# Causal mask of stick-breaking attention: selections on GpSimd instead of mask matmuls

## The chip, the cores and the metric

The kernel runs on one core of a Trainium2 chip. The metric is the device time of one execution in microseconds. The kernel before took 2844.97 us (median of three runs, 2842.08 to 2851.28).

## The reference, cut to what matters

One inference step of a four-layer trunk, width 1024, on 512 prompt frames and 64 sample frames of a running stream (576 rows in all). Layers 0 and 3 mix with stick-breaking attention, layer 1 with a short gated convolution, layer 2 with gated linear attention; each is followed by a squared-ReLU MLP of 4096 hidden units. The change touches stick-breaking attention alone, 16 heads of 64:

```python
z = einsum('bqhd,bkhd->bhqk', q, k) * 64 ** -0.5
mask = k_pos[None, :] < q_pos[:, None]
log_not = where(mask, log_sigmoid(-z), 0.0)
rev = cumsum(log_not, axis=3, reverse=True)          # over the keys
tail = rev shifted by one key, 0 at the end
a = where(mask, exp(log_sigmoid(z) + tail), 0.0)
out = einsum('bhqk,bkhd->bqhd', a, v)
```

So the mask is needed twice: a masked key adds nothing to the sums over later keys, and its own weight is zero. The prompt attends to itself causally; the 64 sample queries attend to 256 cached keys and causally to their own 64.

## The kernel before, in words

Everything is kept in one program with an instruction order written out by hand for each engine; semaphores order the engines among themselves. Each engine executes its list in order. Projections (line 387) split both operands in a high and a low part and use three matmuls for each product; they take most of the time.

**Units of attention.** Each of the two stick-breaking layers works through 24 units: 8 pairs of heads, and for each pair three blocks of 128 keys, newest first. Unit u has pair u // 3. The index u mod 3 gives the block: 0 is key block 2 with, side by side, key block 3 and the sample's own keys (448 columns of queries a head); 1 is key block 1 and the two cached key blocks (512 columns); 2 is key block 0 (512 columns). A tile of a unit holds keys on the 128 partitions and the queries of both heads side by side in columns, so 896 or 1024 columns. Only the first 128 columns of a unit hold its diagonal block, plus columns 256 to 448 in a unit with u mod 3 = 0 (key block 3's diagonal and the sample's).

**The steps of a unit.**

- `scores` (lines 436 to 468, TensorE): the mask matmuls write minus 1e30 where the key isn't before the query (`masked`, line 444: identity times `maskb`, in bf16), and the scores of queries and keys are added to them in PSUM (`scored`, line 451). It waits until ScalarE has read the PSUM tile's former unit (`a_ready` of u - 3).
- `exponents` and `logs` (lines 865 to 877, ScalarE): exp(z), then ln(1 + e).
- `softplus` (lines 1203 to 1217, VectorE): a clamp that yields the softplus value (line 1209), the high part by a copy in fp32r (line 1213), the low part by a subtraction (line 1215); for u mod 3 = 0 also five small instructions on the newer keys (lines 1222 to 1232).
- `cumulative` (line 477, TensorE): matmuls with triangular and all-ones matrices subtract the sums over later keys from the scores in PSUM. Its high half waits for `sp_hi`, its low half for `sp_lo`.
- `weights` (line 885, ScalarE): exp of the result, into the same SBUF tile; it signals `a_ready`.
- `weighted_values` (line 510, TensorE): values times weights; it waits for `a_ready`.
- `output` (lines 889 and 1237), once a pair: ScalarE's copy and VectorE's low part of the result.

**The order.** TensorE's loop (lines 555 to 560) is scores(k + 2), cumulative(k), weighted_values(k - 1). ScalarE's (lines 910 to 918) is weights(k - 1), output when a pair is done, logs(k + 1), exponents(k + 2). VectorE goes through softplus(u) and puts the output of a pair behind unit 1 of the next. Ahead of the loop TensorE transposes the cached keys (four batches) and the values (ten), and VectorE and ScalarE copy them out in turn.

**GpSimd.** In `stick_breaking` (lines 1641 to 1650) it has three DMAs to issue: the cached values at the start, and the stores of V once all batches are copied. Outside it, it adds squares for the norms (line 1613), makes constants, and works in the convolution and the linear attention.

Of the kernel before, what the change touches and what calls it, by code (L numbers as in the profile page):

```python
# [23 lines left out]
ALU = mybir.AluOpType  # L24
ACT = mybir.ActivationFunctionType

P = 128
# [29 lines left out]
UNITS = 3 * PAIRS  # L57
# [16 lines left out]
def first_slab(layer):  # L74
    return layer * LAYER_SLABS
# [7 lines left out]
def trunk(nc, x_prompt, x_sample, cache_sb_k, cache_sb_v, state_conv, state_gla, norm_mix, norm_mlp, sb_w_qkv, sb_w_o,  # L83
          conv_w_in, conv_w, conv_w_out, gla_w_in, gla_w_gk2, gla_b_gk, gla_norm, gla_w_o, mlp_w_up, mlp_w_down,
          norm_final, y_prompt, y_sample, sb_k_p, sb_v_p, sb_k_s, sb_v_s, conv_p, conv_s, gla_p, gla_s):
    with ExitStack() as ctx:
# [3 lines left out]
        def sem(name):  # L90
            return ctx.enter_context(nc.semaphore(name))
# [8 lines left out]
        big = sb("big", [P, 3 * KC, T], F32)  # L100
# [3 lines left out]
        identb = sb("identb", [P, P], BF16)  # L104
# [3 lines left out]
        maskb = sb("maskb", [P, 192], BF16)  # L108
# [56 lines left out]
        sp_hi, sp_lo, r_ready, a_ready, av_done = (sem(n) for n in ("sp_hi", "sp_lo", "r_ready", "a_ready", "av_done"))  # L165
        nw_sum, nw_hi, nw_lo = sem("nw_sum"), sem("nw_hi"), sem("nw_lo")
# [200 lines left out]
        def _(pe):  # L367
# [64 lines left out]
            def stick_breaking(layer, sb_index):  # L432
# [3 lines left out]
                def scores(u):  # L436
                    p, b, z = u // 3, 2 - u % 3, zduo[u % 3]
                    if u >= 3:
                        pe.wait_ge(a_ready, first + u - 2)
                    if u == 1:  # L440
                        pe.wait_ge(sbt_v, tb // 2 + 1)

                    def masked(e, lo, hi, start):
                        pe.matmul(z[:, e, lo:hi], identb[:], maskb[:, 0:hi - lo], start=start, stop=False,  # L444
                                  skip_group_check=True)

                    def scored(lo, hi, keys, q_lo):
                        for e in range(2):
                            r = slice(HD * e, HD * e + HD)
                            k = keys(r)  # L450
                            mm = pe.matmul(z[0:k.shape[1], e, lo:hi], k, big[r, p, q_lo:q_lo + hi - lo], start=False,  # L451
                                           stop=False, skip_group_check=True)
                        return mm

                    for e in range(2):
                        masked(e, 0, P, True)
                        if b == 2:
                            masked(e, 256, 448, False)
                    if b == 2:
                        scored(0, 256, lambda r: big[r, 8 + p, 256:384], 256)  # L460
                        scored(256, 384, lambda r: big[r, 8 + p, 384:512], 384)
                        scored(384, 448, lambda r: big[r, 8 + p, 512:576], 512).then_inc(z_ready, 1)
                    elif b == 1:
                        scored(0, 384, lambda r: big[r, 8 + p, 128:256], 128)
                        scored(384, 448, lambda r: CKT[r, p, 0:128], 512)
                        scored(448, 512, lambda r: CKT[r, p, 128:256], 512).then_inc(z_ready, 1)
                    else:
                        scored(0, 512, lambda r: big[r, 8 + p, 0:128], 0).then_inc(z_ready, 1)
# [27 lines left out]
                def weighted_values(u):  # L496
                    p, b, a = u // 3, 2 - u % 3, weighted(u)
                    pe.wait_ge(a_ready, first + u + 1)
# [598 lines left out]
        def _(dve):  # L1097
# [102 lines left out]
            def stick_breaking(layer, sb_index):  # L1200
                first = UNITS * sb_index

                def softplus(u):
# [6 lines left out]
                    dve.wait_ge(sp_ready, first + u + 1)  # L1210
# [357 lines left out]
        def _(pool):  # L1568
# [72 lines left out]
            def stick_breaking(layer, sb_index):  # L1641
                evacuated = (BATCHES + KBATCHES) // 2 * sb_index

                pool.wait_ge(chunk_done, 2 * (first_slab(layer) + IN_SLABS) + 3)
                pool.dma_start(CV, cache_sb_v[sb_index, 0].rearrange("(j p) h d -> p j (h d)", p=P)).then_inc(cv_in, 16)
                pool.wait_ge(sbt_v, evacuated + BATCHES // 2)
# [3 lines left out]
                pool.dma_start(sb_v_s[sb_index, 0].rearrange("p h d -> p (h d)"), VT[0:TS, 4, :]).then_inc(kv_stored, 16)  # L1650

# [141 lines left out]
```

## Time and profile before

| | us |
|---|---|
| median of three runs | 2844.97 |
| lowest, highest | 2842.08, 2851.28 |
| profiled execution | 2856.15 |
| its span | 2854.4 |
| TensorE busy | 2811.0 (98%) |
| VectorE busy | 1283.1 (45%) |
| ScalarE busy | 862.5 (30%) |
| GpSimd busy | 220.6 (8%) |
| first attention stage | 176.3 to 299.4 |
| second attention stage | 2248.3 to 2371.4 |

In the profile PE is TensorE's matmuls, PEld its weight loads, DVE is VectorE, ACT ScalarE, POOL GpSimd, SP the engine that issues most DMAs. L444 is line 444 of the kernel. Times in the timeline are microseconds from the start of the span. A busy share over the whole span is a mean over stages that have different limits, so the attention stages have to be read by themselves.

### The profile page before, as it was taken

The page shows a single profiled execution, that of the slowest core. Times are in us where ns is not written, and L with a number is a line of the kernel's source. Part 1 is how long each engine was busy: PE and PEld are TensorE (multiplying, and loading weights), DVE is VectorE, ACT ScalarE, POOL GpSimd, SP SyncE. Part 2 cuts the span into 40 slices and gives each one's busy share as a digit, 9 for nine tenths or more (in the row PEclk, how much of TensorE's full clock was granted, in tenths as well). Part 3 has the DMA queues.
Part 4 walks back from the last instruction along what each step waited for, and adds up shares of the span by engine and source line. Part 5 has one row for each costly group of instructions (what it writes and reads, how often), then busy time and mean ns, then how long its engine had stood idle before and what let it go on. Part 6 is the DMA issues. An engine that isn't in the chain of part 4 may idle for free.

```text
span 2854.4 us, 48946 instructions
## 1 busy us (share of the span) xinstructions
PE 2811.0 (98%) x20946; PEld 2726.8 (96%) x20946; DVE 1283.1 (45%) x1721; ACT 862.5 (30%) x945; POOL 220.6 (8%) x223
## 2 busy tenths in 40 slices
PE   8999999999999999999999999999999999999998
PEld 8986999999999999999999899999999869999998
DVE  4358443333455433334467543433443485433333
ACT  3136332222311322223224432222321363322222
POOL 3000100000111100000133110000010001000001
PEclk9999999999999999999999999999999999999999
DMA  4210232222222222222212122222232102322221
GB/s 153 75 62 1 89 118 78 89 74 89 74 89 74 89 86 77 86 77 89 75 46 73 53 74 89 75 88 82 81 103 74 63 1 89 108 88 81 82 81 56
DMA packets 205497, 223.42 MB, mean 78 GB/s; under 512 B 3750, under 2 KB 200464, under 8 KB 205360
## 3 DMA queue, kind: packets, MB, share of 16 engines
q1 hardware_dynamic: 200992, 206.06, 22.4%
q0 software_dynamic: 4368, 15.38, 1.6%
q8 instruction: 105, 1.72, 0.3%
q14 instruction: 32, 0.26, 0.0%
HBM read 208.56 MB, written 12.86 MB: 78 GB/s over the span
## 4 chain that ended last, share of the span: by engine, by line
PE 96%; ACT 2%; DVE 1%; issue 0%; DMA 0%; ACTq 0%; DVEq 0%
PE bank L387 86%; PE bank L477 3%; PE bank L451 2%; PE bank L621 1%; ACT big L885 1%; PE bank L510 1%; PE bank L444 1%; PE bank L675 0%; PE bank L658 0%; PE bank L573 0%; PE bank L539 0%; PE bank L404 0%; PE bank L674 0%; DVE wlo L1104 0%; PE bank L586 0%; ACT e L885 0%
## 5 line engine op out<-in xcount | busy, mean ns | idle before, releaser
L387 PE MATMUL bank<-ahi,whi 128*128 128x288 f32 x3584 | 773.1, 297 | 7.2 <-DVE alo L1129 7.2
L387 PE MATMUL bank<-alo,whi 128*128 128x288 f32 x3584 | 769.4, 296 | 0.0
L387 PE MATMUL bank<-ahi,wlo 128*128 128x288 f32 x3584 | 768.8, 296 | 0.0
L771 ACT ACTIVATE whi<-raw 128x2048 fp32r<-128x2048 f32 x191 | 364.6, 1909 | 834.3 <-PE bank L387 834.3
L387 PEld LDWEIGHTS bank<-ahi,whi 128*128 128x128 f32 x3584 | 579.8, 189 | 9.3 <-DVE wlo L1104 7.3
L387 PEld LDWEIGHTS bank<-alo,whi 128*128 128x128 f32 x3584 | 579.9, 189 | 0.0
L387 PEld LDWEIGHTS bank<-ahi,wlo 128*128 128x128 f32 x3584 | 579.5, 189 | 0.0
L387 PE MATMUL bank<-hhi,whi 128*128 128x288 f32 x2560 | 550.1, 296 | 1.6 <-DVE hlo L1470 1.6
L387 PE MATMUL bank<-hhi,wlo 128*128 128x288 f32 x2560 | 548.1, 296 | 0.0
L387 PE MATMUL bank<-hlo,whi 128*128 128x288 f32 x2560 | 548.0, 296 | 0.0
L1104 DVE TENSOR_TENSOR wlo<-raw,whi 128x2048 fp32r<-128x2048 f32 x192 | 442.2, 2303 | 202.6 <-ACT whi L771 199.9
L387 PEld LDWEIGHTS bank<-hhi,whi 128*128 128x128 f32 x2560 | 412.5, 189 | 3.5 <-issue 3.4
L387 PEld LDWEIGHTS bank<-hhi,wlo 128*128 128x128 f32 x2560 | 412.8, 189 | 0.0
L387 PEld LDWEIGHTS bank<-hlo,whi 128*128 128x128 f32 x2560 | 412.7, 189 | 0.0
L1514 DVE TENSOR_TENSOR X<-bank,X 128x288 f32 (+1 forms) x320 | 131.7, 453 | 490.6 <-PE bank L387 490.5
L1066 ACT ACTIVATE big<-big 128x576 f32<-128x576 f32 x128 | 87.7, 685 | 547.4 <-DVE big L1531 547.4
L1531 DVE SCALAR_TENSOR_TENSOR big<-bank,rstd 128x288 f32<-128x288 f32 x256 | 105.2, 453 | 230.9 <-PE bank L387 230.8
L1535 DVE TENSOR_TENSOR hlo<-big,hhi 128x576 f32 (+1 forms) x128 | 97.2, 759 | 182.5 <-ACT hhi L1067 182.5
L1177 DVE TENSOR_TENSOR big<-bank,rstd 128x288 f32<-128x288 f32 x152 | 62.4, 452 | 205.4 <-PE bank L387 205.1
L1609 POOL MEMSET big<- 128x576 f32 x8 | 4.6, 578 | 1692.2 <-PE bank L387 1692.2
L802 ACT ACTIVATE ahi<-X,vec (+1 forms) x64 | 49.0, 776 | 243.6 <-DVE X L1514 243.5
L1613 POOL TENSOR_TENSOR big<-big 128x576 f32<-128x576 f32 x63 | 97.7, 1551 | 290.0 <-ACT big L805 290.0
(271 smaller groups left out, 1685.1 us busy)
## 6 DMA issues: line engine op xcount, KB each, us to landing
raw<-in_mlp_w_up SPq DMA_DIRECT2D x64, 1024.0 KB, 5.3
raw<-in_mlp_w_down SPq DMA_DIRECT2D x64, 1024.0 KB, 5.0
raw<-in_sb_w_qkv SPq DMA_DIRECT2D x24, 1024.0 KB, 5.2
raw<-in_conv_w_in SPq DMA_DIRECT2D x12, 1024.0 KB, 5.1
raw<-in_gla_w_in SPq DMA_DIRECT2D x12, 1024.0 KB, 5.4
raw<-in_sb_w_o SPq DMA_DIRECT2D x8, 1024.0 KB, 5.1
out<-mixs POOLq DMA_DIRECT2D x2, 2048.0 KB, 7.7
out<-big POOLq DMA_DIRECT2D x2, 2048.0 KB, 8.2
```

What stands on the lines that cost most here:

```text
L387: mm = pe.matmul(acc[h][:, 0:HALF], w[:, u, k, m * P:(m + 1) * P], a[:, k, h * HALF:(h + 1) * HALF], start=(k == 0 and w is whi and a is a ...
L451: mm = pe.matmul(z[0:k.shape[1], e, lo:hi], k, big[r, p, q_lo:q_lo + hi - lo], start=False, stop=False, skip_group_check=True)
L477: return pe.matmul(z[:, e, lo:hi], sums[:, which, :], src, start=False, stop=False, skip_group_check=True)
L771: act.activation(whi[:, 1 - u], raw[:, 1 - u], ACT.Copy).then_inc(w_hi, 1)
L802: act.activation(at(ahi, j), at(X, j), ACT.Copy, scale=g).then_inc(xg_hi, 1)
L1066: act.activation(sq_h[m], relu_t[m], ACT.Square).then_inc(hid_sq, 1)
L1104: dve.tensor_tensor(wlo[:, u], raw[:, u], whi[:, u].bitcast(F32), ALU.subtract).then_inc(w_lo, 1)
L1177: ins = dve.tensor_tensor(dst, acc, rstd[:, hs], ALU.mult)
L1514: ins = dve.tensor_tensor(part(X, j, hs), bank[2 * m + h][:, 0:HALF], part(X, j, hs), ALU.add)
L1531: ins = dve.scalar_tensor_tensor(relu_t[m][:, hs], bank[2 * m + h][:, 0:HALF], 0.0, rstd[:, hs], ALU.max, ALU.mult)
L1535: dve.tensor_tensor(at(hlo, c), sq_h[m], at(hhi, c).bitcast(F32), ALU.subtract).then_inc(hid_ready, 1)
L1613: pool.tensor_tensor(ssq, ssq, sq_x, ALU.add).then_inc(ssq_add, 1)
```

## The change

The mask matmuls go. The scores of a unit start the accumulation themselves, unmasked. GpSimd sets the masked elements to zero instead, twice a unit, in place, with `affine_select` on the diagonal blocks of both heads: once on the softplus values, between VectorE's line 1209 and line 1213, and once on the weights, between `weights` and `weighted_values`. Two semaphores are new, `sp_masked` and `a_masked`. The scores go on waiting for `a_ready`. The constant `maskb` is still made.

```diff
@@ TensorE, scores
-                    def masked(e, lo, hi, start):
-                        pe.matmul(z[:, e, lo:hi], identb[:], maskb[:, 0:hi - lo], start=start, stop=False,
-                                  skip_group_check=True)
...
-                    for e in range(2):
-                        masked(e, 0, P, True)
-                        if b == 2:
-                            masked(e, 256, 448, False)
                     if b == 2:
-                        scored(0, 256, lambda r: big[r, 8 + p, 256:384], 256)
+                        scored(0, 256, lambda r: big[r, 8 + p, 256:384], 256, True)
...
@@ TensorE, weighted_values
-                    pe.wait_ge(a_ready, first + u + 1)
+                    pe.wait_ge(a_masked, first + u + 1)
@@ VectorE, softplus
                     dve.scalar_tensor_tensor(s, s, LN_MAX, zduo[u % 3][:, :, 0:w], ALU.min, ALU.max).then_inc(sp_ready, 1)
-                    dve.wait_ge(sp_ready, first + u + 1)
+                    dve.wait_ge(sp_masked, first + u + 1)
@@ GpSimd, stick_breaking
+                def causal(u, done):
+
+                    blocks = [(0, P), (256, 384), (384, 448)] if u % 3 == 0 else [(0, P)]
+                    for lo, hi in blocks:
+                        v = weighted(u)[:, :, lo:hi]
+                        ins = pool.affine_select(v, v, [[0, 2], [1, hi - lo]], ALU.is_gt, 0.0, base=0, channel_multiplier=-1)
+                    ins.then_inc(done, 1)
+
+                def softplus_mask(u):
+                    pool.wait_ge(sp_ready, UNITS * sb_index + u + 1)
+                    causal(u, sp_masked)
+
+                def weight_mask(u):
+                    pool.wait_ge(a_ready, UNITS * sb_index + u + 1)
+                    causal(u, a_masked)
+
                 pool.wait_ge(chunk_done, 2 * (first_slab(layer) + IN_SLABS) + 3)
                 pool.dma_start(CV, cache_sb_v[sb_index, 0]...).then_inc(cv_in, 16)
+                softplus_mask(0)
+                softplus_mask(1)
                 pool.wait_ge(sbt_v, evacuated + BATCHES // 2)
                 pool.wait_ge(sbt_a, evacuated + BATCHES // 2)
                 pool.dma_start(sb_v_p[sb_index, 0]...).then_inc(kv_stored, 16)
                 pool.dma_start(sb_v_s[sb_index, 0]...).then_inc(kv_stored, 16)
+                weight_mask(0)
+                for u in range(2, UNITS):
+                    softplus_mask(u)
+                    weight_mask(u - 1)
+                weight_mask(UNITS - 1)
```

## Rows read from the trace of the kernel before

**Rows 1.** The page's chain that ended last: share by engine, then by line.

```profile
PE 96%; ACT 2%; DVE 1%; issue 0%; DMA 0%; ACTq 0%; DVEq 0%
PE bank L387 86%; PE bank L477 3%; PE bank L451 2%; PE bank L621 1%; ACT big L885 1%; PE bank L510 1%; PE bank L444 1%; PE bank L675 0%; PE bank L658 0%; PE bank L573 0%; PE bank L539 0%; PE bank L404 0%; PE bank L674 0%; DVE wlo L1104 0%; PE bank L586 0%; ACT e L885 0%
```

**Rows 2.** Line 444's instructions: durations ns min/median/max, first and last start us.

```profile
L444 PE MATMUL bank<-maskb,identb x128: 219/230/246, 176.3 to 2359.3; 128*128 128x128 bf16 x96, 128*128 128x192 bf16 x32
```

**Rows 3.** Busy time by engine of a stage, a pair, a stretch: PE, PEld, DVE, ACT, POOL, clock.

```profile
176.28:299.40 123.12, 117.83 (x856) 82.18 (x856) 95.67 (x133) 78.10 (x93) 2.15 (x3) 0.99 0.11 39
235.85:249.63 13.78, 13.64 (x101) 9.37 (x100) 11.51 (x17) 9.35 (x11) 0.00 (x0) 1.00 0.00 1
186.00:191.00 5.00, 4.65 (x26) 3.98 (x24) 4.33 (x5) 2.35 (x4) 0.00 (x0) 0.66 0.00 2
```

**Rows 4.** Timeline of PE in one pair: start us, duration us, engine, line.

```profile
235.85 0.45 PE L444 MATMUL bank<-maskb,identb 128*128 128x128 bf16 x4
236.24 1.19 PE L451 MATMUL bank<-big 64*128 64x256 f32 x12
...
240.95 0.29 PE L444 MATMUL bank<-maskb,identb 128*128 128x128 bf16 x2
241.17 0.92 PE L451 MATMUL bank<-big 64*128 64x384 f32 x4
```

**Rows 5.** Timeline of DVE in one pair, with idle time before it.

```profile
241.77 1.09 DVE L1209 SCALAR_TENSOR_TENSOR big<-big,bank 128x896 f32<-128x896 f32 x1 [0.97 <-ACT big L877]
...
246.81 1.22 DVE L1209 SCALAR_TENSOR_TENSOR big<-big,bank 128x1024 f32<-128x1024 f32 x1 [0.50 <-ACT big L877]
...
250.43 0.69 DVE L1237 TENSOR_TENSOR hlo<-bank,hhi 128x512 fp32r<-128x512 f32 x1 [0.41 <-ACT hhi L890]
...
255.55 1.09 DVE L1209 SCALAR_TENSOR_TENSOR big<-big,bank 128x896 f32<-128x896 f32 x1 [0.97 <-ACT big L877]
```

**Rows 6.** GpSimd's selections by shape: busy us, mean ns.

```profile
L1599 POOL TENSOR_SCALAR_AFFINE_SELECT mask<-mask 128x128 f32<-128x128 f32 x1 | 0.3, 292 | 0.1
...
L1599 POOL TENSOR_SCALAR_AFFINE_SELECT mask<-mask 128x64 f32<-128x64 f32 x1 | 0.2, 238 | 0.1
```

**Rows 7.** Timeline where ScalarE releases GpSimd.

```profile
307.70 0.67 ACT L805 ACTIVATE big<-X 128x576 f32<-128x576 f32 x1
...
308.45 1.49 POOL L1613 TENSOR_TENSOR big<-big 128x576 f32<-128x576 f32 x1 [1.75 <-ACT big L805]
```

**Rows 8.** Timeline of DVE and POOL side by side, in the gated linear attention's projection.

```profile
1456.49 2.67 POOL L1711 TENSOR_TENSOR stg<-big,stg 128x1152 f32<-128x1152 f32 x1 [2.30 <-ACT stg L933]
...
1457.03 3.36 DVE L1316 TENSOR_TENSOR stg<-big,stg 128x1152 f32<-128x1152 f32 x1
...
1459.12 3.23 POOL L1699 TENSOR_TENSOR stg<-stg 128x1152 f32<-128x1152 f32 x1
...
1484.97 2.65 POOL L1711 TENSOR_TENSOR stg<-big,stg 128x1152 f32<-128x1152 f32 x1 [8.25 <-ACT stg L933]
...
1485.98 2.26 DVE L1400 TENSOR_SCALAR e<-e 128x1152 f32<-128x1152 f32 x1 [2.40 <-ACT e L973]
```

**Rows 9.** Timeline at the start and the end of the first attention stage.

```profile
185.57 1.09 PE L539 MATMUL bank<-ident,big 128*128 128x128 f32 x8 [2.52 <-DVE mixs L1183]
...
187.01 1.91 PE L539 MATMUL bank<-ident,big 128*64 128x128 f32 x8 [0.35 <-DVE mixs L1183]
...
195.92 1.22 POOL L1648 DMA_DIRECT2D out<-mixs  x1 [19.26 <-ACT mixs L845]
...
196.15 0.69 DVE L1213 CAST hlo<-stg 128x1024 fp32r<-128x1024 f32 x1
...
197.13 0.55 POOL L1650 DMA_DIRECT2D out<-mixs  x1
...
200.42 1.09 DVE L1209 SCALAR_TENSOR_TENSOR big<-big,bank 128x896 f32<-128x896 f32 x1 [2.32 <-ACT big L877]
...
294.69 1.23 DVE L1215 TENSOR_TENSOR split_q<-big,split_q 128x1024 fp32r<-128x1024 f32 x1
```

More of the change, by code:

```diff
@@ L165, in trunk @@
         sp_hi, sp_lo, r_ready, a_ready, av_done = (sem(n) for n in ("sp_hi", "sp_lo", "r_ready", "a_ready", "av_done"))
+        sp_masked, a_masked = sem("sp_masked"), sem("a_masked")
         nw_sum, nw_hi, nw_lo = sem("nw_sum"), sem("nw_hi"), sem("nw_lo")
@@ L441, in scores, with scored @@
                         pe.wait_ge(sbt_v, tb // 2 + 1)
-                    def masked(e, lo, hi, start):
-                        pe.matmul(z[:, e, lo:hi], identb[:], maskb[:, 0:hi - lo], start=start, stop=False,
-                                  skip_group_check=True)
-                    def scored(lo, hi, keys, q_lo):
+                    def scored(lo, hi, keys, q_lo, start=False):
                         for e in range(2):
@@ L450, in scored @@
                             k = keys(r)
-                            mm = pe.matmul(z[0:k.shape[1], e, lo:hi], k, big[r, p, q_lo:q_lo + hi - lo], start=False,
+                            mm = pe.matmul(z[0:k.shape[1], e, lo:hi], k, big[r, p, q_lo:q_lo + hi - lo], start=start,
                                            stop=False, skip_group_check=True)
                         return mm
-                    for e in range(2):
-                        masked(e, 0, P, True)
-                        if b == 2:
-                            masked(e, 256, 448, False)
                     if b == 2:
-                        scored(0, 256, lambda r: big[r, 8 + p, 256:384], 256)
+                        scored(0, 256, lambda r: big[r, 8 + p, 256:384], 256, True)
                         scored(256, 384, lambda r: big[r, 8 + p, 384:512], 384)
@@ L463, in scores @@
                     elif b == 1:
-                        scored(0, 384, lambda r: big[r, 8 + p, 128:256], 128)
+                        scored(0, 384, lambda r: big[r, 8 + p, 128:256], 128, True)
                         scored(384, 448, lambda r: CKT[r, p, 0:128], 512)
@@ L467, in scores @@
                     else:
-                        scored(0, 512, lambda r: big[r, 8 + p, 0:128], 0).then_inc(z_ready, 1)
+                        scored(0, 512, lambda r: big[r, 8 + p, 0:128], 0, True).then_inc(z_ready, 1)
                 def cumulative(u):
```

## The prediction, made before the changed kernel was run

> **What bounds the kernel now.** I read the chain of waits first [rows 1]: 96% of it is TensorE, 86% the projection matmuls of line 387, and only 1% the mask matmuls of line 444. The diff touches nothing outside the two attention stages, so what matters is the limit inside them. The mask matmuls are 128 in number and lie in those two stages [rows 2]; the first stage takes 123.1 us, and a period inside it (one pair of heads, three units) takes 13.78 us, with TensorE busy 13.64, VectorE 11.51, ScalarE 9.35 and GpSimd nothing at all [rows 3]. So TensorE sets the pace of a pair today, by a small margin. I write 0, 1, 2 for a unit by its index modulo 3.
>
> VectorE's margin comes from the timeline of one pair [rows 5]. Its period, softplus to softplus of unit 0, is 255.55 - 241.77 = 13.78 us. In it VectorE waits 0.50 + 0.41 + 0.97 = 1.88 us, for ScalarE's logarithms and for its copy of the output. That leaves 13.78 - 1.88 = 11.90 us of work that VectorE must issue in order. This 11.90 is the number on which the case turns.
>
> **The change part by part.** *Removed: mask matmuls.* In each pair TensorE loses four before unit 0's scores and two before each other unit's. From start to start that is 236.24 - 235.85 = 0.39 us and 241.17 - 240.95 = 0.22 us, the last twice (unit 2's look the same) [rows 4]: 0.83 us a pair, 13.3 us over 16 pairs. TensorE's period would be 13.78 - 0.83 = 12.95 us, if TensorE stayed the one that sets it. The scores still wait for the unmasked weights, so nothing is added in front of them.
>
> *Added: the selections' own time.* GpSimd took 0.292 us for 128 columns and 0.238 for 64 [rows 6]: 0.054 us for 64 more columns, 0.184 fixed. A block of both heads is 256 columns: 0.184 + 4 x 0.054 = 0.40 us. Units 1 and 2 have one block; unit 0 has two and one of 2 x 64 columns, 0.40 + 0.40 + 0.29 = 1.10 with rounding. That is 1.90 us a pair for the softplus values and 1.90 for the weights. Upper end: if 256 columns cost twice 0.292, 0.58 + 0.58 + 1.46 = 2.6 us. Lower end: 0.238 for each of five, 1.2 us. I take 1.90, the line through the two rows.
>
> The Trainium skill (GPSIMD Engine Reference, section on elementwise work, side-by-side cycle accounting) states 1.8 cycles at 1.2 GHz, 1.5 ns, an element for a one-input loop. Laid on the fixed 0.184 that gives 0.57 us for 256 columns and 2.7 for the pair's softplus masks instead of 1.9, some 2890 us for the kernel, the case C below. It would also give 0.38 us for 128 columns where the row shows 0.29, so here the row decides.
>
> *Added: a wait inside VectorE's softplus.* The copy to the high part (line 1213) now waits for GpSimd, which waits for line 1209. VectorE is in order: behind the waiting copy stand the low part, unit 0's five newer-key instructions, the output's low part and the next softplus; nothing fills the hole. So the 1.90 us are not hidden under VectorE's other work, they are added to it. Two hand-overs come with each unit: an instruction of ScalarE that ended at 308.37 released GpSimd at 308.45, 0.08 us [rows 7]; for the way back I estimate 0.04, about what separates an ending ScalarE instruction from the next engine. Of this 0.03 is spent already between lines 1209 and 1213. 3 x 0.09 = 0.27 us a pair. Ends: 0 to 0.6.
>
> *Added: the two engines on one path to SBUF.* GpSimd started a two-input instruction at 1456.49 that ended at 1459.16; VectorE's began at 1457.03 and took 3.36 us, 1.23 of it after that end; GpSimd's next, of 3.23 us, ran 1.96 of them after VectorE's end at 1460.39 [rows 8]. They took turns, each held for the whole of the other. A VectorE instruction with one input, 1152 columns, was held too: begun at 1485.98, done 0.62 us after GpSimd's end at 1487.62 [rows 8]. The masks of the weights fall in this trap. GpSimd's order is softplus mask of u, weight mask of u - 1. In the pace of VectorE the weights of u - 1 are done when the softplus mask of u ends: TensorE's last sums and ScalarE's exponential take about 2.3 us behind the low part of u - 1, and VectorE needs as long or longer (1.25 for line 1209, then the mask). So the weight mask starts just as the high copy of u is released, and the copy waits 0.40 us behind it in two of three units; for unit 0's three selections, taking turns, both the copy and the low part wait, 0.8. Full price 1.6 us a pair; nothing if VectorE wins each race. I take 1.3, near the full price, because GpSimd's next instruction follows without a gap (1459.12 on an end at 1459.16). Ends: 0 to 2.6.
>
> *The new period.* 11.90 + 1.90 + 0.27 + 1.30 = 15.4 us, over TensorE's 12.95 and over today's 13.78. ScalarE's 9.35 fits. VectorE then waits for nobody else: after the low part of a unit, last sums, exponential and logarithm take 3.3 us, and VectorE has at least 4.8 to do (output, softplus with its mask, copies). The 0.83 us taken from TensorE are worth nothing here.
>
> *Start of a stage.* TensorE's transposes wait for VectorE there (2.52 us) [rows 9], and softplus of units 0 and 1 stands in front of the copies that free them. The first mask costs 1.10 + 0.09, less 0.39 of mask matmuls: +0.8; the second +0.5. Then unit 2: GpSimd first issues the stores of V (1.22 + 0.55 us from 195.92, now from 197.2 to 199.0), then unit 0's weight mask (1.10), and only then unit 2's softplus mask, to 200.5. The high copy, today at 196.15, comes at 200.55, its low part ends at 202.5, and unit 3's softplus, today at 200.42 after 2.32 us idle [rows 9], begins at 202.5: +2.1 us. That idle time absorbs the rest of the delay.
>
> *The seven periods after it.* From 200.42 to the end of the last low part (294.69 + 1.23 = 295.92 [rows 9]) there are 95.5 us today, with seven pairs of softplus. New: 7 x 15.4 = 107.8, +12.3. *End:* the last weight mask is in the open, 0.40 + 0.12 = +0.5.
>
> *Sum.* 12.3 + 2.1 + 0.5 = 14.9 us a stage, 29.8 for two. The profiled execution took 2856.15 us (span 2854.4, 1.75 around it); it would take 2886, +1.04%. On the median of 2844.97, from which I count, that is 2875 us.
>
> **The rivals.** *A: VectorE wins the race, or the selections do not hold it.* For it: the two sides start within 0.1 us of each other. Against: [rows 8]. Period 14.07, so 3.0 + 2.1 + 0.5 = 5.6 us a stage, 2856 us.
>
> *B, the other side: VectorE's idle time swallows the masks and TensorE keeps the pace.* Place: the hole between lines 1209 and 1213. The whole saving of 0.83 us a pair then counts, 13.3 us, less 2 us of start: 2834 us. It decides at a period of 12.95, which is 1.05 us of stall a pair; five selections at 0.2 and three hand-overs already exceed this. No change within my bound would need 1.4 to 2.0 us of stall in all; the selections and hand-overs alone are 2.2. Only VectorE's 1.88 us of idle speak for it, and they are counted.
>
> *C: the selections over the two heads cost 256 columns at the full double price.* 2.6 us for the stall and half of its extra for collisions: period 16.4 to 16.7, about 22 to 24 us a stage, 2890 us.
>
> *D: TensorE's clock falls.* With 12.95 us of work in 15.4 it gets gaps. At the start of the stage the granted clock was 0.66 in 5 us [rows 3] after a pause of TensorE; inside a pair it was 1.00. Eight transposes took 1.91 us there instead of 1.09 [rows 9], on its way between 1.2 and 2.4 GHz; at that ratio, 1.75, a pair of 12.95 takes 22.7. If a third of the pairs ran so, 5 x 7.3 = 37 us more, 2912 us. Against: the new gaps are of about 0.8 us, three a pair, and today's of 0.2 leave it whole.
>
> **How the numbers follow.** Forecast 0.52, A 0.22, B 0.04, C 0.14, D 0.05, others 0.03. A measurement here tells about 0.3% (8.5 us) from nothing. Faster: B, 0.04. Same: a third of A with shorter selections, and strays, 0.09. Slower 0.87. The range goes from A to the midst of C's far side: 2854 to 2898.
>
> **What would show it.** In the changed trace, inside a stage: a period of 15.4 us; VectorE idle between lines 1209 and 1213 for 1.2 us in unit 0 and 0.5 in the others, released by GpSimd; selections of 0.40 us in the hole and longer ones behind it; line 1213's mean above 0.69; TensorE waiting on VectorE's parts at line 477 and no longer on ScalarE at the scores; granted clock 1.00. Wrong would be: VectorE still idle for ScalarE (rival B), line 1213 at 0.69 (A), selections of 0.58 (C). Outside the stages nothing should move by more than 1 us.

## The result, and the profile after

The changed kernel took 2868.88 us (median of eight runs, 2856.72 to 2872.13), the kernel before 2852.81 us (eight runs, 2841.6 to 2860.74) on the same chip: ratio 1.0056, 95% interval 1.0032 to 1.008. It is slower by 0.56%, about 16 us. The forecast was slower, by 1.04% or 29.8 us, so the difference that came is about half of it; the forecast time, 2875 us, lies 6 us above what came. The profiled execution of the changed kernel took 2869.93 us, with a span of 2868.2, that is 13.8 more than the 2854.4 of before.

The chain that ended last, from the page of the changed kernel; it answers to [rows 1]:

```profile
PE 90%; DVE 6%; issue 1%; POOL 1%; ACT 1%; DMA 0%; ACTq 0%; POOLq 0%; DVEq 0%
```

TensorE's share fell from 96 to 90%, and VectorE's rose from 1 to 6%: VectorE is now the limit inside the two attention stages. (In the kernel after, the lines of the attention's engines stand 7 lower: the clamp is line 1202, the high copy 1206, the low part 1208, the first newer-key instruction 1215, the sums 470, the weighted values 503, the logarithms 870, the weights 878. The selections are line 1642.)

Who waited for the selections of line 1642, by the view of that line (us, times):

```profile
  DVE whi L1206: 17.1, 24
  DVE hlo L1206: 8.3, 6
  DVE split_r L1206: 7.5, 10
  DVE split_q L1206: 5.3, 8
```

38.2 us in 48 waits of VectorE between clamp and high copy, in the two stages. The same hole in one pair, by VectorE's timeline; it answers to [rows 5]. The bracket is the idle time before an instruction and who ended it:

```profile
243.96 1.07 DVE L1202 SCALAR_TENSOR_TENSOR big<-big,bank 128x896 f32<-128x896 f32 x1
246.15 0.63 DVE L1206 CAST whi<-big 128x896 fp32r<-128x896 f32 x1 [1.12 <-POOL big L1642]
...
247.82 0.63 DVE L1215 TENSOR_TENSOR raw<-big 128x256 f32<-128x256 f32 x1
...
249.69 1.21 DVE L1202 SCALAR_TENSOR_TENSOR big<-big,bank 128x1024 f32<-128x1024 f32 x1
251.41 0.87 DVE L1206 CAST whi<-big 128x1024 fp32r<-128x1024 f32 x1 [0.51 <-POOL big L1642]
252.32 1.30 DVE L1208 TENSOR_TENSOR wlo<-big,whi 128x1024 fp32r<-128x1024 f32 x1
...
254.28 1.20 DVE L1202 SCALAR_TENSOR_TENSOR e<-e,bank 128x1024 f32<-128x1024 f32 x1
256.00 0.69 DVE L1206 CAST split_q<-e 128x1024 fp32r<-128x1024 f32 x1 [0.51 <-POOL e L1642]
256.72 1.31 DVE L1208 TENSOR_TENSOR split_q<-e,split_q 128x1024 fp32r<-128x1024 f32 x1
257.95 1.07 DVE L1202 SCALAR_TENSOR_TENSOR big<-big,bank 128x896 f32<-128x896 f32 x1
```

Three things are to be seen. The period is 257.95 - 243.96 = 13.99 us, where it was 13.78 [rows 5]. All waits for ScalarE are gone; the only idle time left is 1.12 + 0.51 + 0.51 = 2.14 us, and all of it is GpSimd's. And a few instructions are longer than they were: the copy takes 0.87 in one unit where it took 0.69, the first newer-key instruction 0.63 where it took 0.42.

GpSimd's side of the same pair, by its timeline (a row can hold several selections, x3 or x4, with their time together):

```profile
245.10 1.01 POOL L1642 TENSOR_SCALAR_AFFINE_SELECT big<-big 128x256 f32<-128x256 f32 x3 [2.14 <-DVE big L1202]
246.85 1.31 POOL L1642 TENSOR_SCALAR_AFFINE_SELECT big<-big 128x256 f32<-128x256 f32 x1 [0.74 <-ACT big L878]
250.97 2.81 POOL L1642 TENSOR_SCALAR_AFFINE_SELECT big<-big 128x256 f32<-128x256 f32 x4 [2.80 <-DVE big L1202]
255.55 0.41 POOL L1642 TENSOR_SCALAR_AFFINE_SELECT e<-e 128x256 f32<-128x256 f32 x1 [1.77 <-DVE e L1202]
256.13 0.82 POOL L1642 TENSOR_SCALAR_AFFINE_SELECT big<-big 128x256 f32<-128x256 f32 x1 [0.17 <-ACT big L878]
```

A selection on 2 x 128 columns takes 0.41 us while VectorE stands still (the row of 255.55), three of unit 0 take 1.01. Beside VectorE's copies and low parts the same ones take 0.82 and 1.31.

Busy time by engine of the same pair, and of a stretch at the end of the first stage (columns: length, PE, PEld, DVE, ACT, POOL, granted clock, DMA share, GB/s); they answer to [rows 3]:

```profile
243.96:257.95 13.99, 13.07 (x94) 8.96 (x93) 11.68 (x17) 9.27 (x12) 6.37 (x10) 1.00 0.00 0
295.00:300.00 5.00, 4.99 (x28) 3.77 (x27) 4.40 (x6) 1.02 (x1) 2.33 (x3) 0.66 0.00 0
```

TensorE now has 0.9 us of idle time in a pair and keeps its full clock in it. At the end of the stage it doesn't: the granted clock of that stretch is 0.66.

**Where the 13.8 us are.** I measure a stage from GpSimd's issue of the cached values' DMA to its first constant after the stage, since both stand in its list before and after. The first stage went from 130.19 to 135.27 us (+5.08), the second from 130.46 to 137.21 (+6.75). Its parts, by VectorE's rows: start (DMA to the clamp of unit 3) +1.54 and +1.83; from there to the end of the last low part 97.99 and 98.00 where it was 95.50 in both, +2.49 and +2.50; the rest, end of the stage, 11.26 and 12.63 us where it was 10.21 in both, +1.05 and +2.42. Together +11.83. The other 2.0 us arose in layer 2, which the change doesn't touch: between the two constants of GpSimd that stand around it (1337.31 and 1638.88 in the trace of before) lie 301.57 us before and 303.48 in the changed kernel, and over the twelve traces of this case 299.3 to 304.1 us, in no order that follows the masks. In 23 runs of the kernel before that went beside the experiments the whole time lay between 2834.24 and 2860.24, so single total times tell little here, and the experiments are read by the length of stage and period in their traces.

### The profile page after: what moved, and what is told of

It reads as the page before. It is cut to its first block, busy times and chain, and to the rows that moved or that the text cites. A ratio compares the mean times of both kernels' runs of the same rounds, so it can differ in the third digit from the quotient of the medians.

```text
span 2868.2 us, 48850 instructions
## 1 busy us (share of the span) xinstructions
PE 2807.5 (98%) x20818; PEld 2725.2 (95%) x20818; DVE 1285.4 (45%) x1721; ACT 861.5 (30%) x945; POOL 316.2 (11%) x383
## 4 chain that ended last, share of the span: by engine, by line
PE 90%; DVE 6%; issue 1%; POOL 1%; ACT 1%; DMA 0%; ACTq 0%; POOLq 0%; DVEq 0%
PE bank L388 86%; DVE big L1202 1%; PE bank L614 1%; POOL big L1642 1%; DVE whi L1206 1%; DVE wlo L1208 0%; PE bank L470 0%; DVE e L1202 0%; PE bank L668 0%; PE bank L651 0%; PE bank L566 0%; DVE raw L1215 0%; DVE hlo L1230 0%; PE bank L405 0%; DVE split_r L1206 0%
```

## The experiments

The theory going in was the prediction's with smaller sizes: VectorE's list sets the pace; a period is its work, plus the holes in which it waits for GpSimd, plus what the weight selections hold it up. The rivals were that TensorE's clock or order, or GpSimd's own length, sets the 13.99.

### No selections at all (x_none)

Takes the waits and all selections out of the changed kernel, so nothing is masked:

```diff
-                    pe.wait_ge(a_masked, first + u + 1)
+                    pe.wait_ge(a_ready, first + u + 1)
-                    dve.wait_ge(sp_masked, first + u + 1)
+                    dve.wait_ge(sp_ready, first + u + 1)
-                softplus_mask(0) ... weight_mask(UNITS - 1)
```

> The changed kernel without any selection: neither softplus values nor weights are masked, no engine waits for GpSimd; the output lacks the causal mask. It shows what the removed mask matmuls are worth alone. Theory (VectorE's in-order work with the hole for the selections sets the changed kernel's pace; without the hole TensorE sets it): period of a pair 12.95 us (13.78 less 0.83), stage about 123.1 - 6.6 = 116.5 us. Rival (the score matmuls get no cheaper, or ScalarE sets the pace through the weights): period within 0.2 of 13.78.

Measured: period 12.97 us (12.95 to 12.98 over both stages), stages 124.25 and 124.51 us, that is 5.9 less than before in each; 2847.32 us in one run. VectorE's timeline of one pair:

```profile
239.39 1.09 DVE L1202 SCALAR_TENSOR_TENSOR big<-big,bank 128x896 f32<-128x896 f32 x1 [0.57 <-ACT big L870]
...
244.21 1.22 DVE L1202 SCALAR_TENSOR_TENSOR big<-big,bank 128x1024 f32<-128x1024 f32 x1 [0.28 <-ACT big L870]
...
247.62 0.69 DVE L1230 TENSOR_TENSOR hlo<-bank,hhi 128x512 fp32r<-128x512 f32 x1 [0.20 <-ACT hhi L883]
...
252.36 1.09 DVE L1202 SCALAR_TENSOR_TENSOR big<-big,bank 128x896 f32<-128x896 f32 x1 [0.58 <-ACT big L870]
```

VectorE waits for ScalarE again, as before, and TensorE is busy 55.35 us of the 56 from 215 to 271: it sets the pace. So the 0.83 us of mask matmuls a pair were sized rightly (13.78 - 12.95), and they are worth 12 us over two stages (260.65 - 248.76 = 11.9) if nothing takes the matmuls' place. The selections cost 23.7 us over this (272.48 - 248.76).

### The softplus values' selections alone (x_softplus)

The weights stay unmasked: `weight_mask` isn't called, and `weighted_values` waits for `a_ready`.

> The changed kernel with the softplus selections only; the weights aren't masked, so no selection runs beside VectorE's copies. Theory: VectorE still sets the pace, and the period falls from 13.99 by what the collisions with the weight selections cost, 0.55 us as line 1206, 1208 and 1215 grew: 13.44 us; line 1206 at 0.69, line 1208 at 1.23 again. Rival (the collisions cost the 1.3 us of the prediction): 12.95, TensorE's own pace.

Measured: period 13.45 us (13.44 to 13.46), stages 130.91 and 130.56, 2856.25 us in one run. VectorE's timeline of one pair:

```profile
237.91 1.08 DVE L1202 SCALAR_TENSOR_TENSOR big<-big,bank 128x896 f32<-128x896 f32 x1
240.10 0.63 DVE L1206 CAST whi<-big 128x896 fp32r<-128x896 f32 x1 [1.12 <-POOL big L1642]
...
241.77 0.42 DVE L1215 TENSOR_TENSOR raw<-big 128x256 f32<-128x256 f32 x1
...
243.09 0.43 DVE L1225 TENSOR_TENSOR split_r<-raw,split_r 128x256 fp32r<-128x256 f32 x1
243.44 1.21 DVE L1202 SCALAR_TENSOR_TENSOR big<-big,bank 128x1024 f32<-128x1024 f32 x1
245.16 0.69 DVE L1206 CAST whi<-big 128x1024 fp32r<-128x1024 f32 x1 [0.51 <-POOL big L1642]
245.89 1.23 DVE L1208 TENSOR_TENSOR wlo<-big,whi 128x1024 fp32r<-128x1024 f32 x1
...
251.35 1.08 DVE L1202 SCALAR_TENSOR_TENSOR big<-big,bank 128x896 f32<-128x896 f32 x1
```

Every instruction has its old length again (0.69, 1.23, 0.42), the holes are the same 2.14 us. So VectorE's own work issued back to back is 13.45 - 2.14 = 11.31 us, not 11.90, and the weight selections' effect on VectorE in the changed kernel is 13.99 - 13.45 = 0.54 us a pair. The lengthened instructions give the same: +0.18 (copy of unit 1), +0.08 and +0.08 (low parts of units 1 and 2), +0.21 (line 1215), in all 0.55. The whole is then 11.31 + 2.14 + 0.55 = 14.00.

### The weights' selections alone (x_weights)

The other half: the softplus values stay unmasked, the copy waits for the clamp alone, and GpSimd's list after the stores is `for u in range(UNITS): weight_mask(u)`.

> The changed kernel with the weight selections only; the softplus values aren't masked and VectorE has no hole. Theory: the weight selections have slack of 2.7 to 4 us before TensorE needs them, so they cost nothing: period 12.95 us like the kernel without selections, although VectorE's copies are held a little. Rival (the collisions, or TensorE's wait for masked weights, set the pace): 13.5 us or more.

Measured: period 12.95 to 12.99 us, the first one 13.8; stages 126.36 and 126.35; 2842.09 us in one run. That is TensorE's pace: the selections of the weights cost a period nothing while VectorE has time to spare, and what they add to the path from weights to values is hidden. The stages are 2.1 and 1.8 us longer than in x_none all the same: 0.7 and 0.4 at the start (24.53 and 24.55 us from the DMA to the clamp of unit 3, 23.83 and 24.11 without them), 0.9 in the one longer period and behind it, and 0.5 at the end, where the last selection is in the open.

### Twice the softplus selections (x_double)

Ahead of each selection of softplus values the same selections once more, into an unused tile:

```diff
                 def softplus_mask(u):
                     pool.wait_ge(sp_ready, UNITS * sb_index + u + 1)
+                    for w in (P, P, TS) if u % 3 == 0 else (P,):
+                        made(pool.affine_select(conv_y[:, 0:2 * w]..., negones[:, 0:w]..., [[0, 2], [1, w]], ...))
                     causal(u, sp_masked)
```

> The changed kernel with, before each softplus selection, one more of the same size by GpSimd on scratch. It doubles the hole. Theory: everything GpSimd adds between lines 1202 and 1206 is added to the period: four times 0.36 + 0.08 and once 0.25 + 0.08, so 2.1 us a pair: period 16.1, stage about 128.2 + 7 x 2.1 + 2 = 145 us; TensorE gets gaps of over 1 us in each unit, and its clock may fall in some. Rival (there is slack that absorbs part, as the small rise of 0.21 us a pair suggests): period under 15.5.

Measured: period 16.14 to 16.37 us, stages 154.65 and 153.58, 2895.82 us in one run. VectorE's copies:

```profile
242.32 0.80 DVE L1206 CAST whi<-e 128x896 fp32r<-128x896 f32 x1 [2.43 <-POOL e L1642]
...
248.03 0.87 DVE L1206 CAST hlo<-big 128x1024 fp32r<-128x1024 f32 x1 [0.99 <-POOL big L1642]
...
```

The third copy of the pair waits 0.99 us too. The holes grew from 2.14 to 2.43 + 0.99 + 0.99 = 4.41 us, and the period by about as much (2.2 to 2.4): what GpSimd does between clamp and copy comes through to the period in full. Over the changed kernel's stages these are 19.4 and 16.4 us more, where 16.7 were expected; of the 19.4, 15.8 lie in the pairs, 2.6 at the start (28.6 against 26.02) and 1.0 at the end. From 215 to 271 the mean granted clock was 0.88 here, where it is 1.00 in the changed kernel: rival D exists, but with longer pauses of TensorE (up to 1.44 us, at 248.96) than the change makes inside a pair (0.79).

### Hiding the selection under the clamp (x_split)

The clamp is cut in two, the columns with the diagonal blocks first; GpSimd masks them while VectorE clamps the others.

```diff
-                    dve.scalar_tensor_tensor(s, s, LN_MAX, zduo[u % 3][:, :, 0:w], ALU.min, ALU.max).then_inc(sp_ready, 1)
+                    near = slice(256, w) if u % 3 == 0 else slice(0, P)
+                    rest = slice(0, 256) if u % 3 == 0 else slice(P, w)
+                    for part_, done in ((near, sp_ready), (rest, sp_rest)):
+                        dve.scalar_tensor_tensor(s[:, :, part_], s[:, :, part_], LN_MAX, zduo[u % 3][:, :, part_],
+                                                 ALU.min, ALU.max).then_inc(done, 1)
+                    dve.wait_ge(sp_rest, first + u + 1)
```

> The changed kernel with VectorE's softplus (line 1202) cut in two: the columns of the diagonal block first, GpSimd is released, and the rest of the columns while GpSimd selects. In unit 0 the columns 256 to 448 go first and the block 0 to 128 is selected last. Theory (the hole is VectorE waiting, nothing else): the hole goes from 0.51 to about 0 in units 1 and 2 and from 1.12 to about 0.5 in unit 0; three more instructions cost some 0.3 us; VectorE's period 13.99 - 2.14 + 0.5 + 0.3 = 12.7, under TensorE's 12.97, so the period is 12.97 to 13.1 and the stage some 126 to 128 us from the DMA of line 1654 to the memset of line 1602 (changed kernel 135.3 and 137.2, before 130.2). Kernel about 8 us faster than before. Rival (GpSimd and VectorE also hold each other up during line 1202, or GpSimd's selections now fall on copies): period stays near 14.

Measured: 2848.91 us (median of ten), ratio to the kernel before 0.9989, interval 0.9968 to 1.001; stages 125.54 and 126.55 us. VectorE's timeline of one pair (line 1205 is the clamp, 1211 the copy):

```profile
240.17 1.15 DVE L1205 SCALAR_TENSOR_TENSOR big<-big,bank 128x384 f32<-128x384 f32 x2 [0.52 <-ACT big L870]
241.89 0.63 DVE L1211 CAST whi<-big 128x896 fp32r<-128x896 f32 x1 [0.57 <-DVE big L1205]
...
245.34 1.28 DVE L1205 SCALAR_TENSOR_TENSOR big<-big,bank 128x256 f32<-128x256 f32 x2
246.70 0.69 DVE L1211 CAST whi<-big 128x1024 fp32r<-128x1024 f32 x1
...
253.12 1.15 DVE L1205 SCALAR_TENSOR_TENSOR big<-big,bank 128x384 f32<-128x384 f32 x2 [0.51 <-ACT big L870]
```

The two pieces of the clamp take 1.28 us together where one took 1.21. The hole has gone in units 1 and 2 and is 0.57 in unit 0, where the copy comes 0.09 us after GpSimd's three selections end (the row names the clamp; the selections ran from 240.79 to 241.80). The period is 253.12 - 240.17 = 12.95: TensorE's, as in the prediction. The two stages are 20.4 us shorter than in the changed kernel and 8.6 shorter than in the one before. This shows the hole to be the cause of the slowdown: the same selections in the same number cost 3.3 us over the two stages (252.09 against 248.76 without any) where they cost 23.7, once VectorE doesn't stand still for them, and what is left lies at the start and the end of a stage. In the total the gain over the kernel before is not told from no change by the interval.

### The start of a stage (x_start)

`softplus_mask(2)` and `weight_mask(0)` go ahead of the two stores of V in GpSimd's list.

> The changed kernel with unit 2's softplus mask and unit 0's weight mask put ahead of the two DMAs that store V in GpSimd's order. Theory: at the start of a stage VectorE waited 2.55 us before line 1206 of unit 2; with this it waits 0.51, but unit 3's softplus then waits for ScalarE's logarithm (about 1.3 us after the low part), so about 1.0 to 1.3 us less a stage. Rival: the start is set by ScalarE and TensorE and nothing changes (under 0.3 us).

Measured: from the DMA to the clamp of unit 3, 25.67 and 25.68 us where the changed kernel has 26.02 and 26.58; stages 136.2 and 134.2; 2870.75 us in one run. VectorE's rows at the start, first of the changed kernel, then of this one:

```profile
199.87 0.70 DVE L1206 CAST hlo<-stg 128x1024 fp32r<-128x1024 f32 x1 [2.55 <-POOL stg L1642]
...
201.96 1.07 DVE L1202 SCALAR_TENSOR_TENSOR big<-big,bank 128x896 f32<-128x896 f32 x1
```

```profile
199.05 0.87 DVE L1206 CAST hlo<-stg 128x1024 fp32r<-128x1024 f32 x1 [0.51 <-POOL stg L1642]
...
202.58 1.09 DVE L1202 SCALAR_TENSOR_TENSOR big<-big,bank 128x896 f32<-128x896 f32 x1 [1.32 <-ACT big L870]
```

The wait behind the stores was real (2.55 us) and is gone (0.51), but ScalarE's logarithm is late next, so of about 2 us only 0.35 and 0.9 are gained, less than the 1.0 to 1.3 expected. The stage lengths differ by more because of the ends: in the first stage the clock was low there (0.64 in the stretch 300 to 305) and the end took 12.66 us, in the second it stayed at 1.00 and the end took 10.68.

### Work in TensorE's pause at the end (x_fill)

Twelve matmuls of 192 columns that nobody reads, ahead of the sums of unit 22, where the changed kernel's TensorE pauses:

```diff
+                    if k == UNITS - 2:
+                        pe.wait_ge(a_ready, first + UNITS - 2)
+                        for i in range(12):
+                            pe.matmul(zduo[0][:, i % 2, 0:192], identb[:], maskb[:], start=True, stop=False, ...)
```

> The changed kernel with twelve matmuls of 192 columns that nobody reads, put by TensorE into its pause ahead of the last sums of unit 22, where no scores are left. Theory (the pause at the end of a stage lets the granted clock fall to 0.66 and less in the next 5 to 10 us, which costs the tail 0.6 us in the first stage and 2.7 in the second): granted clock 1.00 in the last 15 us of both stages, the stage 0.5 to 2.5 us shorter, 134.7 in both. Rival (the tail is long because of the chain of selections and exponentials, the clock doesn't matter): no change.

TensorE's timeline at that place, of the changed kernel and of this one:

```profile
291.28 1.08 PE L503 MATMUL bank<-big,mixs 128*64 128x512 f32 x4
294.34 0.50 PE L470 MATMUL bank<-split_q,sums 128*128 128x512 f32 x1 [1.98 <-DVE split_q L1206]
```

```profile
292.32 1.16 PE L554 MATMUL bank<-maskb,identb 128*128 128x192 bf16 x12
294.28 0.50 PE L470 MATMUL bank<-split_q,sums 128*128 128x512 f32 x1 [0.80 <-DVE split_q L1211]
```

And this kernel's windows there:

```profile
295.00:300.00 5.00, 4.33 (x31) 3.25 (x30) 4.42 (x6) 1.02 (x1) 1.94 (x3) 1.00 0.00 0
```

Measured: clock 1.00 in the stretch where it was 0.66, with the pause cut from 1.98 us to 0.80. Stages 134.88 and 135.45, that is 0.4 and 1.8 us less; 2863.46 us in one run; period 13.99, unchanged. The ends take 10.71 and 10.69 us where they took 11.26 and 12.63, so the low clock cost 0.55 of the end's +1.05 and 1.94 of its +2.42; the remaining 0.5 is the last selection.

That the pause brings the low clock fits this run, but it doesn't do so each time. In the second stage of x_start TensorE paused just as long,

```profile
2376.38 0.50 PE L470 MATMUL bank<-split_q,sums 128*128 128x512 f32 x1 [1.96 <-DVE split_q L1206]
```

and the granted clock was 1.00 from 2375 to 2385. Over the 24 stages of the twelve traces, ten have a pause of 1.49 to 2.81 us at this place, and the clock fell behind seven of them; the other fourteen have none over 0.80 us, and it fell in none. What decides among the ten is open.

### All three together (x_all)

The edits of x_split, x_start and x_fill in one kernel.

> The three edits together: split softplus, GpSimd's order at the start, filling matmuls. Theory: period 12.97, start as in the start experiment, clock 1.00 at the end: stage 125 us instead of 130.2 before, so about 10 us (0.35%) faster than the kernel before and 24 us faster than the changed one. Rival: the edits overlap and it stays within 3 us of the split alone.

Measured: 2848.96 us (median of twelve), ratio to the kernel before 0.9977, interval 0.9954 to 1.0. Stages 125.82 and 126.11, sum 251.93, against 252.09 for x_split alone: the rival came true. The new order at the start still gains there, 0.6 and 1.3 us (24.53 and 24.80 us to the clamp of unit 3, 25.13 and 26.09 in x_split), but the pairs behind it take 0.5 us more (90.2 against 89.7) and the end 0.4 more (11.07 against 10.68): with the hole gone TensorE's pause there is 0.34 us in x_split, the granted clock from 290 to 305 is 1.00 in both, and the filling matmuls only take time. It beats the changed kernel by 20.6 us in its stages, and the one before by 8.7; of the latter the total shows 0.2%, at the edge of what can be told.

### The mask matmuls put back (x_keep)

The changed kernel with the mask matmuls of before added again, so that everything is masked twice. It asks what the removed 0.83 us of TensorE are worth.

> The changed kernel with the mask matmuls put back, so everything is masked twice. Theory (in the changed kernel VectorE sets the pace, so TensorE's 0.83 us a pair are worth nothing there): period 14.0 us, as in the changed kernel, since TensorE's 13.78 still fit under it; the stage within 1 us of the changed kernel's, but for 0.4 us at its start. Rival (the removal brought its 0.83 us and hides part of the selections' cost): period 14.8.

Measured: period 13.74 to 13.79 us, stages 133.83 and 133.63, 2863.76 us in one run. Neither I nor the rival had this: with more work on TensorE the period is 0.2 us shorter than the changed kernel's 13.99. (The stages are shorter by 1.4 and 3.6 us; 1.5 of that is the pairs, 0.6 and 1.9 the ends, where the clock stayed at 1.00.) GpSimd's and VectorE's timelines of one pair (line 1650 is the selections, 886 the weights, 1214 the copy, 1226 the second newer-key instruction):

```profile
236.73 0.41 POOL L1650 TENSOR_SCALAR_AFFINE_SELECT big<-big 128x256 f32<-128x256 f32 x1 [2.47 <-DVE big L1210]
237.57 2.16 POOL L1650 TENSOR_SCALAR_AFFINE_SELECT e<-e 128x256 f32<-128x256 f32 x3 [0.42 <-ACT e L886]
```

```profile
237.18 0.69 DVE L1214 CAST hlo<-big 128x1024 fp32r<-128x1024 f32 x1 [0.51 <-POOL big L1650]
237.91 1.30 DVE L1216 TENSOR_TENSOR hlo<-big,hlo 128x1024 fp32r<-128x1024 f32 x1
...
247.68 0.49 DVE L1226 CAST split_r<-big 128x256 fp32r<-128x256 f32 x1
```

The holes are the same 1.12, 0.51 and 0.51, but the weights are ready later (the selections of unit 0 wait 0.42 us for ScalarE, where they follow at once in the changed kernel), the copy of unit 1 is through before they begin (0.69, not 0.87), and unit 2's low part is not met (1.23). What is left of the collisions is 0.08 + 0.21 = 0.29, and 11.31 + 2.14 + 0.29 = 13.74. TensorE, at 13.78, keeps step. That the later weights are the reason fits these rows; no run moved the weights alone, so it isn't shown. What is shown, by one run with two stages, is that taking the mask matmuls off TensorE brought nothing within this order of work.

### Twice the weight selections (x_wdouble)

As in x_double, but the extra selections stand ahead of those of the weights.

> The changed kernel with, before each weight selection, one more of the same size on scratch, so twice as many of GpSimd's instructions fall beside VectorE's copies; the hole is as before. Theory (each of them holds VectorE for its data phase only, the first ones for 0.1 to 0.2 us, which made 0.55 us a pair for five selections): 0.55 us more, period 14.5 us. Rival 1 (each costs VectorE its whole 0.36 us, as the prediction had it): 15.6. Rival 2 (the extra selections push the next softplus mask back, as GpSimd works in order): a hole longer than 1.12 and 0.51 us before line 1206.

Measured: period 14.19 us where 14.5 was expected, stages 140.89 and 138.17, 2878.08 us in one run. (The stages mix in a start that is 1.3 and 1.0 us longer, and the clock at the end: it fell in the first, where the end took 14.50 us, and not in the second, 11.16.) GpSimd had 34.62 us of work in the 56 from 215 to 271 instead of 25.47, and the period grew by 0.20. The holes stayed at 1.11, 0.51 and 0.51. One of VectorE's rows shows the reason:

```profile
250.25 0.49 DVE L1218 CAST split_r<-big 128x256 fp32r<-128x256 f32 x1
```

One instruction more is held, by 0.21 us (0.49 where it took 0.28). The whole length of a selection, as the prediction charged it, is the wrong price: VectorE pays 0.08 to 0.21 us for each copy or subtraction of its own, with all operands in SBUF, that begins under a selection. And the clamp pays nothing. In the changed kernel it never meets a selection; here 27 clamps do, and neither side is longer:

```profile
255.93 1.01 POOL L1642 TENSOR_SCALAR_AFFINE_SELECT big<-big 128x256 f32<-128x256 f32 x3
256.37 1.20 DVE L1202 SCALAR_TENSOR_TENSOR e<-e,bank 128x1024 f32<-128x1024 f32 x1
```

## Why the prediction was right, and where its sizes were off

Right was the mechanism with its sign: VectorE becomes the limit through the hole between clamp and copy, the removed matmuls are worth nothing, and 2868.88 lies in the range. The size was 2.5 times too large in the stages: 29.8 us forecast, 11.8 measured. That the total came within 6 us owes something to the base: counted on the 2852.81 that the kernel before took beside it, and not on 2844.97, the same sum would have said 2883. As a difference, rival A's 11 us was nearer to the 16 measured than the forecast's 29.8. By its terms:

| term | forecast | measured |
|---|---|---|
| TensorE's period without mask matmuls | 12.95 | 12.95 to 12.98 (x_none) |
| selections and hand-overs in the hole | 1.90 + 0.27 = 2.17 | 2.14 |
| VectorE's work in order | 11.90 | 11.31 (x_softplus) |
| collisions | 1.30 | 0.55 |
| period | 15.4 | 14.0 |
| start of a stage | +2.1 | +1.54, +1.83 |
| unit 3 to the last low part | +12.3 | +2.49, +2.50 |
| end of a stage | +0.5 | +1.05, +2.42 |

**The hole** was sized to 0.03 us: 0.41 a block (forecast 0.40), 1.01 for three (1.10), hand-overs of 0.10 to 0.11 a unit. The law drawn through two rows of another shape [rows 6] held.

**The work in order, 0.59 us too much.** "13.78 - 1.88 = 11.90" takes the printed idle times off the period. But an instruction that waits for nobody starts before the one ahead has ended: the clamp of 243.44 in x_softplus begins 0.08 us before 243.09 + 0.43, while that of 244.21 in x_none begins its printed 0.28 behind the end of the same forerunner. Taking 0.28 off leaves the lost 0.08 in the period, and this step of the prediction failed too, by half a microsecond. Start to start, the same steps of a pair are 0.60 us shorter in x_softplus: 0.08 or 0.09 at each of three places where VectorE had waited for ScalarE, 0.21 from line 1231 to the clamp (0.34 to 0.13), and 0.04 to 0.05 behind each clamp. The first are an overlap that waiting destroys. The 0.21 is that and a short wait that the profile doesn't print: in the trace of before the clamp of 251.37 comes 0.12 us behind the end of its forerunner and 0.03 behind the end of ScalarE's logarithm (250.28 + 1.06). For the last I have only the rows.

**The collisions, 0.75 us too much.** This is the step that failed most: the term of 1.30, by which the copy waits for a whole selection of 0.40 us in two of three units and copy and low part 0.8 for unit 0's three. In kind "they took turns" [rows 8] holds here too. A selection that begins under a copy or a low part ends behind it, never before: 256.95 against the copy's 256.69, 248.16 against the low part's 247.90, 253.78 against 253.62. And where VectorE is second, it waits for the selection:

```profile
251.33 0.41 POOL L1642 TENSOR_SCALAR_AFFINE_SELECT big<-big 128x256 f32<-128x256 f32 x1
```

The copy of 251.41, in the rows of the pair above, begins 0.08 us behind it. This copy ends 0.54 us after the selection; alone it takes 0.69. So 0.15 us of it ran under the selection. The held instruction of line 1215 ends at 248.45, 0.29 after the selection's 248.16; alone it takes 0.42, so 0.13 ran under it. The rows of the prediction say the same: of the instructions held there, one ended 1.23 us after GpSimd's and takes 1.34 when not held, the other 0.62 and takes 0.75.

Two things were mis-sized, then. GpSimd is mostly second: only the selection of 251.33 starts ahead of VectorE's instruction, by 0.08 us, while the others begin under one and pay for it themselves, stretched from 0.41 to 0.82, 0.86 and 1.31 us and from 0.30 to 1.27. And what VectorE then pays is not a selection, but what is left of it when the next copy or subtraction begins (0.33, 0.23, 0.23 and 0.34 us), less the 0.13 to 0.15: 0.18 + 0.08 + 0.08 + 0.21 = 0.55 us a pair. That these 0.15 us are a start-up which doesn't need the other's turn is read off the rows; no run isolates it. Rival A (no collisions, period 14.07, 5.6 us a stage) came nearest in numbers (14.0, 5.08 and 6.75), by two errors that cancel: the collisions exist, and the work in order was smaller.

The Trainium skill ("SBUF — State Buffer", section "Who interferes with whom") says that of a VectorE instruction in a two-port mode, or with two inputs in SBUF, and a GpSimd instruction, the second to issue is fully blocked until the first has finished. The trace agrees: the selection of 256.13, second to the copy of 256.00, took 0.82 us instead of 0.41 and ended behind it, and the copy of 251.41, second to a selection, ended 0.54 us after it. What the rows add is the price, 0.18 us for that copy and not the 0.41 of the selection.

**The seven periods.** Of the 9.8 us a stage that this term was too large, 7 x 1.37 = 9.6 come from the sizes above. A smaller point: "+0.21 a period" would give 7 x 0.21 = 1.5 and not 2.49, because the last pair had been shorter than the others: TensorE has no scores of later units left there, so before it took 95.50 - 6 x 13.78 = 12.82 us, and now, at VectorE's pace, 97.99 - 6 x 14.00 = 13.99.

**The start** was right in kind (the copy of unit 2 waits 2.55 us behind GpSimd's stores and unit 0's weights), and 0.3 to 0.6 too long: the first store took 0.78 us instead of 1.22 [rows 9], so the copy came at 199.87 and not 200.55.

**The end** was right in its 0.5 (TensorE waits 0.56 for the last selection of the weights), and missed the clock. Rival D was put inside the pairs, where the clock stayed at 1.00; it came true only at the last pair, where nothing else fills the 1.98 us pause.

**Rival C** has a slip that decides nothing: at twice 0.292 and twice 0.238 us its five selections take 2.8 us and not 2.6.

## What to carry to other kernels

A helper engine between two instructions of an engine that works in order adds its whole length to that engine's list, and what goes beyond the list's spare time lengthens the period: put the piece that the helper needs first, and let the rest of the instruction run over it. Before taking work from the engine that paces, work out how much the second one has to spare, from its starts and not from its printed idle times: here VectorE's list took 11.31 us beside the 12.95 left to TensorE, 1.64 to spare, and was given 2.69. Ask of each meeting of two engines which comes second, and charge it what is left of the first, not the first's whole length.

## What was not expected of the hardware

- A selection of GpSimd and a copy or subtraction of VectorE with all operands in SBUF take turns, and the second pays. A selection that comes second ends 0.15 to 0.27 us behind VectorE's instruction (0.41 us becomes 0.82, 0.86, 1.31). An instruction of VectorE that comes second lost 0.18 us (copy of 1024 columns), 0.08 (subtraction of 1024) or 0.21 (256 columns), and ended its own length less 0.13 to 0.15 us after the selection.
- The clamp and the output's low part, which read one operand from PSUM, were not lengthened by selections beside them and didn't lengthen them (1.20 and 0.68 us beside three that took 1.01, in x_wdouble).
- An instruction of VectorE that waits for nobody starts about 0.08 us before the one ahead of it has ended; one that waits loses this.
- TensorE's granted clock fell to 0.66 in a stretch of 5 us behind a pause of 1.98 us (between 1.2 and 2.4 GHz), and in the second stage to 0.58 and then 0.74; with the pause cut to 0.80 us it stayed at 1.00. But it also stayed at 1.00 behind pauses of 1.96 us (x_start) and 2.16 us (x_wdouble), each in the second stage. Inside the pairs of the changed kernel TensorE is idle 0.9 us in 14.0, 0.79 of them in one pause, and the clock stayed at 1.00.
- The issue of the same store took GpSimd 1.22 us before and 0.78 us after: 1.22 in the three traces where it comes 19 us after GpSimd's last work (before, x_none, x_weights), 0.78 in the others, where selections stand closer ahead of it.
